# Two-layer hybrid attention model: the second score products of large sparse units on 64 rows, the two heads on different row halves

## The reference

```
ls = jnp.einsum('bqghd,bgqnd->bghqn', qg, k_sel) * scale
ps = masked_softmax(ls, tok_mask[:, :, None])
o_slc = jnp.einsum('bghqn,bgqnd->bqghd', ps.astype(v_sel.dtype), v_sel)
...
lw = jnp.einsum('bqghd,bkgd->bghqk', qg, kw) * scale
pw = masked_softmax(lw, mw)
```

## Time and profile before

| | |
|---|---|
| median of 3 runs | 1343.29 us (1343.28 to 1344.05) |
| the profiled execution | 1341.39 us |
| its span, first to last instruction | 1339.6 us |
| TensorE busy | 1277.3 us, 95% of the span |
| VectorE busy | 693.1 us, 52% |
| ScalarE busy | 657.6 us, 49% |
| mean granted TensorE clock | 0.994 of full speed |

### The profile page before, as it was taken

One profiled execution on the slowest core, in us unless ns is written; L12 is line 12 of the kernel. 1 busy time (PEld: TensorE's weight loads), 2 busy tenths in 40 slices (PEclk: granted clock), 3 DMA queues, 4 the chain that ended last, 5 costly groups with the idle time before them and its releaser, 6 DMA issues.

```text
span 1339.6 us, 18513 instructions
## 1 busy us (share of the span) xinstructions
PE 1277.3 (95%) x6626; PEld 1050.0 (78%) x6626; DVE 693.1 (52%) x1194; ACT 657.6 (49%) x1222; POOL 66.1 (5%) x153
## 2 busy tenths in 40 slices
PE   5999988999999999999999999889999999999995
PEld 4997666788888888788889867667888888887884
DVE  6435666445555555433363457672555555554333
ACT  4336788534545444322352478882454454543222
POOL 1004110001000000000000310100000000000000
PEclk9999999999999999999999999999999999999998
DMA  6320100124333333322133210012223333323211
GB/s 216 106 88 15 65 1 33 48 63 123 94 94 95 99 102 101 107 94 93 51 106 92 63 64 1 1 51 91 80 80 103 99 96 94 94 94 110 94 47 63
DMA packets 121480, 107.56 MB, mean 80 GB/s; under 512 B 3874, under 2 KB 110980, under 8 KB 121424
## 3 DMA queue, kind: packets, MB, share of 16 engines
q1 hardware_dynamic: 119200, 102.71, 25.0%
q0 software_dynamic: 1360, 3.45, 0.9%
q10 hardware_dynamic: 864, 0.66, 0.2%
HBM read 104.71 MB, written 2.10 MB: 80 GB/s over the span
## 4 chain that ended last, share of the span: by engine, by line
PE 87%; DVE 6%; ACT 4%; issue 1%; DMA 1%; SPq 0%; DVEq 0%
PE ps L1370 24%; PE ps L1372 24%; PE ps L1371 24%; PE ps L1597 4%; PE ps L1550 4%; PE ps L1531 2%; DMA raw<-in_w_in_dram 1%; PE ps L1537 1%; DVE probs L1032 1%; PE ps L1536 1%; DVE x L1052 1%; DVE probs L1151 1%; ACT probs L836 1%; DVE w_lo L569 1%; PE ps L1609 1%
## 5 line engine op out<-in xcount | busy, mean ns | idle before, releaser
L1370 PE MATMUL ps<-ht_hi,w_hi 128*128 128x512 f32 (+2 forms) x776 | 297.2, 383 | 2.5 <-DVE w_lo L569 2.5
L1372 PE MATMUL ps<-ht_hi,w_lo 128*128 128x512 f32 (+2 forms) x776 | 295.9, 381 | 0.0
L1371 PE MATMUL ps<-ht_lo,w_hi 128*128 128x512 f32 (+2 forms) x776 | 295.9, 381 | 0.0
L569 DVE TENSOR_TENSOR w_lo<-raw,w_hi 128x1024 fp32r<-128x1024 f32 (+4 forms) x196 | 218.8, 1140 | 102.5 <-ACT w_hi L562 92.2
L562 ACT ACTIVATE w_hi<-raw 128x1024 fp32r<-128x1024 f32 (+4 forms) x196 | 187.2, 982 | 100.9 <-PE ps L1372 97.2
L1315 DVE SCALAR_TENSOR_TENSOR conv<-ps,cols,conv 128x510 f32<-128x510 f32 (+1 forms) x176 | 127.7, 746 | 179.8 <-ACT conv L957 173.9
L1370 PEld LDWEIGHTS ps<-ht_hi,w_hi 128*128 128x128 f32 x776 | 145.8, 188 | 31.2 <-DVE w_lo L569 3.0
L1371 PEld LDWEIGHTS ps<-ht_lo,w_hi 128*128 128x128 f32 x776 | 145.9, 188 | 28.2 <-issue 0.5
L1372 PEld LDWEIGHTS ps<-ht_hi,w_lo 128*128 128x128 f32 x776 | 145.8, 188 | 27.5
L1370 PE MATMUL ps<-w_hi,ht_hi 128*128 128x430 f32 (+1 forms) x392 | 148.0, 378 | 4.9 <-DVE ht_lo L1039 4.2
L957 ACT ACTIVATE conv<-ps,cols 128x512 f32<-128x512 f32 x88 | 68.2, 775 | 159.9 <-PE ps L1372 159.6
(11 more groups left out here) (178 smaller groups left out, 1533.5 us busy)
## 6 DMA issues: line engine op xcount, KB each, us to landing
raw<-in_ffn_w_up_dram SPq DMA_DIRECT2D x88, 512.0 KB, 4.4
raw<-in_ffn_w_down_dram SPq DMA_DIRECT2D x44, 512.0 KB, 3.3
raw<-in_w_in_dram SPq DMA_DIRECT2D x32, 430.0 KB, 3.6
raw<-in_w_out_dram SPq DMA_DIRECT2D x16, 512.0 KB, 3.3
raw<-in_nsa_cmp_w_dram SPq DMA_DIRECT2D x8, 512.0 KB, 3.7
x<-in_x_dram SPq DMA_DIRECT2D x4, 512.0 KB, 6.3
out_dram<-probs SPq DMA_DIRECT2D x4, 512.0 KB, 2.6
raw<-in_mla_w_uq_dram SPq DMA_DIRECT2D x4, 384.0 KB, 2.9
```

The costliest lines, as they stand in the source:

```text
L569: last = nc.vector.tensor_tensor(d(w_lo)[:, :, d0:d1], r(raw)[:, :, r0:r1], d(w_hi)[:, :, d0:d1].bitcast(F32), ALU.subtract)
L1370: mm(o, lhs[0], rhs[0], start=start, stop=False)
L1371: mm(o, lhs[0], rhs[1], start=False, stop=False)
L1372: return mm(o, lhs[1], rhs[0], start=False, stop=stop)
```

## The change

For large sparse units, `scores` now issues the full 128-row product with the high part of the keys for both heads first. After both, it issues the product with the low part of the keys, on the 64 rows that hold the high part of the queries alone: rows 0 to 63 for the even head, rows 64 to 127 for the odd one. The term low of q times low of k is no longer added in these units. Small sparse units and latent units keep their products.

```
--- before.py
+++ after.py
@@ -1526,6 +1526,11 @@
                         if h == 0 or big(u):
                             scores_read(SCORE_BANK[u, h][1])
                         place = score_place(u, h)
+                        if u >= U_MLA and big(u):
+                            head = 2 * (pair - H // 2) + h
+                            c = 4 * (head // GROUP) + 2 * branch
+                            mm(place, qs[:, head, qt], ks[:, c, 0:n], start=True, stop=False)
+                            continue
                         if u < U_MLA:
...
                         else:
                             head = 2 * (pair - H // 2) + h
                             c = 4 * (head // GROUP) + 2 * branch
-                            mm(place, qs[:, head, qt], ks[:, c, 0:n], start=h == 0 or big(u), stop=False)
-                            mm(place, qs[:, head, qt], ks[:, c + 1, 0:n], start=False, stop=h == 1 or big(u))\
+                            mm(place, qs[:, head, qt], ks[:, c, 0:n], start=h == 0, stop=False)
+                            mm(place, qs[:, head, qt], ks[:, c + 1, 0:n], start=False, stop=h == 1).then_inc(sc_done, 1)
+                    if u >= U_MLA and big(u):
+                        for h in range(2):
+                            head = 2 * (pair - H // 2) + h
+                            own = halves(head)[0]
+                            c = 4 * (head // GROUP) + 2 * branch
+                            mm(score_place(u, h), qs[own, head, qt], ks[own, c + 1, 0:n], start=False, stop=True)\
                                 .then_inc(sc_done, 1)
```

## The result

| | before | after |
|---|---|---|
| median | 1342.37 us (6 runs) | 1352.1 us (6 runs, 1351.48 to 1357.98) |
| the profiled execution | 1341.39 us | 1354.2 us |
| its span | 1339.6 us | 1352.4 us |
| mean granted TensorE clock of the profiled execution | 0.994 | 0.991 |

The ratio after to before is 1.0081, with a 95% interval of 1.0062 to 1.0101. The change makes the kernel slower, by about 10 us. The forecast was 5.3 us slower, with a range that ended at 1352.0.

A forecast was written before the change was run, and what follows sets the result against it. TensorE, busy 1277.3 of 1339.6 us, was taken to bound the kernel overall, with VectorE carrying some pairs. Eight pair terms summed to 2.64 us a layer, 5.3 for both, giving 1348.6 us against the median; range 1343.0 to 1352.0.

The forecast's parts named there:

- The overlap: Both heads' half-row products run together, saving one product per unit: 0.17 us in 384-column units, 0.24 in 512-column units.
- The way in: Switching TensorE from 128 to 64 rows before the half-row products: 0.09 + 0.11 = 0.20 us.
- The delay of A's scores: In the 384-column unit, the first head's second product finishes 0.37 us later, and VectorE's first maximum waits for it.
- A: The 384-column unit that opens each group of four sparse units; first of a pair, 8 pairs per layer.
- B's bank wait: 512-column unit's second full product waits for a maximum's bank; second products now stand behind it; pair at 213 us: 0.57 us.
- B: The 512-column unit that follows the 384-column unit in each pair of large sparse units.
- The rival without overlap: Half-row products in the sparse units do not overlap: 3.56 us a layer, 7.1 in all, 1350.4 us; chance 0.14.
- The rival of the free switch: Row switch is free, but the order delays scores: 0.78 us a layer, 1.6 in all, 1344.9 us; chance 0.14.
- The faster rival: Half-row loads run during full products, products overlap, later scores find slack: 6.5 us go, 1336.8 us; chance 0.07.
- both stretches: The sparse units' two stretches of 84 us, one per layer; each was to become 2.6 us longer.
- the signs: Expected in the trace: simultaneous half-row starts, first maximum 0.37 us later, stretches 2.6 us longer, pair at 213 us worst.
- the pair at 167 us: Large sparse units at 167 us: TensorE's wait for ScalarE covers the 384-column unit; -0.24 + 0.20, about -0.03 us.

The follow-up runs named there:

- experiment 9: Kernel before, with the second products of large sparse units on their own 64 rows in the old order; 1351.86 us, ratio 1.0075.
- experiment 2: Changed kernel with both second products on rows 0 to 63, so that they cannot overlap; 1352.23 us, ratio 1.0084.
- experiment 8: Changed kernel with VectorE's normalization moved ahead of the 384-column unit's maxima in sparse groups; 1341.56 us.
- Experiment 3: Changed kernel with five extra 512-column products, results unused, in each of three waits for L1182 per layer; 1347.83 us.
- experiment 11: Kernel before with the same filler of five products in the waits for L1182; 1341.95 us, ratio 0.9999.
- experiment 4: Changed kernel run again unaltered, as control and for a second trace; 1352.17 us.
- Experiment 6: Kernel before with the change in the 384-column units alone; 1352.43 us, ratio 1.0075.
- experiment 1: Changed kernel's order, but second products on all 128 rows, with no shape switch and no overlap; 1348.52 us, ratio 1.0045.
- experiment 12: Kernel before with VectorE's normalization ahead of the maxima only in the three groups per layer that wait for L1182; 1332.81 us, ratio 0.9933.
- 512-column variant: Kernel before with the change in the 512-column units alone, 1348.64 us; the same with the five-product filler, 1343.28 us.

## Why the prediction was wrong

**Right: what the units cost.** The prices were read from rows of before, and they held. The overlap: 0.45 us for both products, 0.62 without it. The way in, 0.20 us: experiment 9 has 0.20 us at each change. The delay of A's scores, 0.37 us: 0.38 in the trace. B's bank wait, into which the first head's second product no longer falls: 0.58 at 213 us for 0.57. The rival without overlap was also priced right: it had 3.56 us a layer, and experiment 2 shows 3.65. The rival of the free switch falls with the 0.20 us of experiment 9. The faster rival falls with experiment 8: with the wait on VectorE gone, the change costs 3.7 us a layer in the units. The Trainium skill's rule in "TensorE: Matmul & The Clock Gate", Part 3, that small products on different row groups run together, is borne out by the 0.45 us. The pull-ahead of weight loads in the same part does not reach across a change from 128 to 64 rows: the load at 204.32 us waited in experiment 9.

**Wrong: a term was missing.** The sentence that failed is the sum itself: "2.64 us a layer, 5.3 us for both. Everything behind the stretches is TensorE work and moves with it." It took the granted clock as given, because it was 1.00 in both stretches of the earlier trace rows. The changed kernel loses it. Nothing in the sum stood for that, and none of the rivals or the signs named it. Experiment 3 gives 4.3 us back with work that does nothing but fill the wait, and experiment 11 shows that the same filler is worth nothing in the kernel before. So of the 10 to 11 us, 5.9 are the units and 4.3 to 4.6 are half-clock stretches that follow the waits for L1182 (4.3 by the filler, 4.6 by the trace of experiment 4). The range ended at 1352.0, 0.1 us short; but against the six runs of the kernel before, the forecast was short by 4.4 us of 9.7.

**Wrong in part: the pair at 167 us.** I had -0.03 and it is 0.25. I covered A with TensorE's own wait for ScalarE and did not follow A's scores on VectorE. There the normalization (L1178) ends at 170.83 us, and the value products wait for it. Before, it was over by 169.69 us, 0.39 us ahead of them. After the change:

```profile
170.14 0.69 DVE L1178 TENSOR_TENSOR onorm<-ps,onorm 128x512 f32<-128x512 f32 x1
...
170.42 0.49 PE L1548 MATMUL ps<-ks,qs 64*128 64x512 f32 x2
...
170.97 1.73 PE L1608 MATMUL ps<-probs_t,vm 128*64 128x256 f32 x16
```

The step from the half-row products to the value products is 0.55 us, where 0.43 (one product in 0.34, then 0.09) would do. The rest, 0.17 us, comes two steps later. Experiment 6 puts the cause on A: with the 384-column units alone this pair costs the same 0.25 us, and with the 512-column units alone it has -0.04.

**What stays open.** What in TensorE's activity decides over the clock is not settled. The length of the wait alone does not tell the kernels apart. The six waits for L1182 last 1.83 us each in the kernel before, and half clock follows none of them. They last as long in experiment 6, and it follows three. They last 1.63 us in the changed kernel, and it follows two or three. Nor does busy time in these rows. The 4.10 us up to the value block had 2.36 us of it in the changed kernel at 203 us, and this much at the same place before, where the clock stayed:

```profile
203.00:207.10 4.10, 2.31 (x15) 1.68 (x13) 3.03 (x8) 2.45 (x7) 0.00 (x0) 1.00 0.00 0
```

What differs is that 11 records stand there instead of 15, and that a half-row product uses half of the array's rows. The clocks in the table would fit thinner work as the cause, but this is not shown: experiment 1, with 128 rows throughout, also had half clock at these waits in its profiled run, and no run varied the idle time by itself. Nor is it settled why half clock comes behind layer 1 and behind layer 2 at waits that both kernels have, in some traces and not in others.

## What to carry to other kernels

A product saved on TensorE has to be set against three things that a count of products leaves out: the change of shape on both sides (0.20 us here on the way in alone, more than the 0.17 us saved), the result that comes later because it was moved behind another head's product, and the waits behind which it now stands. Look for the engine that waits for the first result: here VectorE idled for 2.40 us in front of it, and moving VectorE's other work into that idle time was worth 9 us (experiment 12), while taking work off TensorE cost 10. And where TensorE waits for almost 2 us behind work that was made shorter, ask whether the granted clock holds; a few idle products into a free bank show it in one run.

## What the runs showed of the hardware that was not expected

Products whose results nobody uses made the kernel faster: 1352.17 to 1347.83 us with 30 extra products of 512 columns, and 1348.64 to 1343.28 in the 512-column variant. A half-clock stretch costs 1.35 to 1.63 us behind a wait for L1182. A wait of under 2 us can be followed by one (1.63 us in the changed kernel's row above), in a run with a mean clock of 0.991. A longer wait, 1.84 us in the earlier trace rows, was not.
